# A hybrid decoder step on one core: stick-breaking prompt heads in pairs instead of one by one

## The reference

```python
def sb_attend(q, k, v, q_pos, k_pos, bias):
    z = (jnp.einsum('bqhd,bkhd->bhqk', q.astype(jnp.float32), k.astype(jnp.float32)) * SB_DH ** -0.5
         + bias.astype(jnp.float32)[None, :, None, None])
    valid = (k_pos[None, :] < q_pos[:, None])[None, None]
    log_stay = jnp.where(valid, jax.nn.log_sigmoid(-z), 0.0)
    after = lax.cumsum(log_stay, axis=3, reverse=True) - log_stay
    w = jnp.where(valid, jnp.exp(jax.nn.log_sigmoid(z) + after), 0.0)
    return jnp.einsum('bhqk,bkhd->bqhd', w, v.astype(jnp.float32))
```

## Time and profile before

| | before |
|---|---|
| median of 3 runs | 1431.58 us (1430.72 to 1433.55) |
| the profiled execution | 1428.48 us, of which 1426.7 us is the span from first to last instruction |
| PE busy, PEld busy | 91%, 87% of the span |
| DVE, ACT, POOL busy | 42%, 29%, 10% |
| mean granted TensorE clock | 0.935 of 2.4 GHz |
| prompt stick-breaking heads on PE | 600.65 to 697.31 us of the span |
| value products of the samples (L634) | 714.05 to about 741.5 us |

### The profile page before, as it was taken

One profiled execution on the slowest core, in us unless ns is written; L12 is line 12 of the kernel. 1 busy time (PEld: TensorE's weight loads), 2 busy tenths in 40 slices (PEclk: granted clock), 3 DMA queues, 4 the chain that ended last, 5 costly groups with the idle time before them and its releaser, 6 DMA issues.

```text
span 1426.7 us, 22310 instructions
## 1 busy us (share of the span) xinstructions
PE 1305.4 (91%) x9492; PEld 1242.0 (87%) x9492; DVE 604.6 (42%) x630; ACT 412.6 (29%) x462; POOL 149.1 (10%) x154
## 2 busy tenths in 40 slices
PE   5999999999977999889898869689999999999893
PEld 4999999999977999767586649679999999999893
DVE  5444312443345333255438632554442134433744
ACT  5222222222333111254311143432222222222442
POOL 6100000000113000100013301220000000001321
PEclk9999999999988999999857859899999999999997
DMA  5222223221230222201500002202222322222201
GB/s 182 89 88 81 67 89 118 89 88 56 77 134 30 88 88 91 92 30 45 177 0 18 22 10 77 88 30 88 88 74 89 103 89 89 77 68 91 90 30 63
DMA packets 36743, 109.98 MB, mean 77 GB/s; under 512 B 4626, under 2 KB 4642, under 8 KB 36562
## 3 DMA queue, kind: packets, MB, share of 16 engines
q1 hardware_dynamic: 34850, 103.10, 22.0%
q0 software_dynamic: 1232, 5.01, 1.1%
q10 hardware_dynamic: 608, 1.10, 0.2%
HBM read 103.57 MB, written 5.64 MB: 77 GB/s over the span
## 4 chain that ended last, share of the span: by engine, by line
PE 87%; DVE 7%; ACT 2%; issue 2%; POOL 0%; DMA 0%; ACTq 0%; POOLq 0%; DVEq 0%
PE PS L426 72%; PE PS L634 2%; DVE work L1118 2%; PE PS L682 1%; DVE x L1130 1%; PE PS L548 1%; DVE a_lo L1109 1%; PE PS L577 1%; PE PS L740 1%; PE PS L437 1%; PE PS L480 1%; PE PS L533 1%; PE PS L743 1%; PE PS L557 1%; PE PS L574 1%
## 5 line engine op out<-in xcount | busy, mean ns | idle before, releaser
L426 PE MATMUL PS<-a_hi,w_hi 128*128 128x272 f32 (+1 forms) x2064 | 432.6, 292 | 50.2 <-DVE a_lo L1109 22.8
L426 PE MATMUL PS<-a_lo,w_hi 128*128 128x272 f32 (+1 forms) x2064 | 431.3, 291 | 0.0
L426 PE MATMUL PS<-a_hi,w_lo 128*128 128x272 f32 (+1 forms) x2064 | 429.8, 290 | 0.0
L426 PEld LDWEIGHTS PS<-a_hi,w_hi 128*128 128x128 f32 (+1 forms) x2064 | 328.4, 191 | 57.9 <-issue 33.6
L426 PEld LDWEIGHTS PS<-a_hi,w_lo 128*128 128x128 f32 (+1 forms) x2064 | 328.2, 190 | 0.5
L426 PEld LDWEIGHTS PS<-a_lo,w_hi 128*128 128x128 f32 (+1 forms) x2064 | 326.0, 190 | 0.5
L1103 DVE TENSOR_TENSOR w_lo<-raw,w_hi 128x2048 fp32r<-128x2048 f32 (+2 forms) x97 | 201.6, 2078 | 229.5 <-ACT w_hi L803 229.5
L803 ACT ACTIVATE w_hi<-raw 128x2048 fp32r<-128x2048 f32 (+2 forms) x97 | 166.0, 1711 | 115.5 <-PE PS L426 115.4
L426 PE MATMUL PS<-h_lo,w_hi 128*128 128x272 f32 x704 | 145.2, 288 | 0.0
L426 PE MATMUL PS<-h_hi,w_lo 128*128 128x272 f32 x704 | 144.6, 287 | 0.0
L426 PE MATMUL PS<-h_hi,w_hi 128*128 128x272 f32 x704 | 144.5, 287 | 0.0
(11 more groups left out here) (272 smaller groups left out, 1072.2 us busy)
## 6 DMA issues: line engine op xcount, KB each, us to landing
raw<-in_f_in SPq DMA_DIRECT2D x86, 512.0 KB, 4.5
raw<-in_f_out SPq DMA_DIRECT2D x32, 384.0 KB, 3.3
raw<-in_w_in SPq DMA_DIRECT2D x24, 512.0 KB, 4.6
raw<-in_f_out SPq DMA_DIRECT2D x32, 320.0 KB, 3.1
raw<-in_w_out SPq DMA_DIRECT2D x8, 512.0 KB, 4.7
y<-in_cache_sb_k SPq DMA_DIRECT2D x16, 256.0 KB, 2.8
raw<-in_ple_w_gate SPq DMA_DIRECT2D x8, 512.0 KB, 4.6
x<-in_x SPq DMA_DIRECT2D x8, 272.0 KB, 7.1
```

The lines of the kernel that those rows point to most:

```text
L426: last = mm(PS[0:width, 4 * quad + 2 * c + half, 0:HALF], wt[:, slot, cols], act[:, k, half * HALF:(half + 1) * HALF], start=(k == 0 and n ...
```

## The change

Heads are taken in pairs p = 0 to 3.

- Logits: both heads' products read `proj` directly, head 2p in array rows 0 to 63 and head 2p+1 in rows 64 to 127, instruction by instruction in turn, into different banks. A pair's logits come in three units (diagonals; the 384 columns of key block 0; the 256 and 128 columns of blocks 1 and 2), and the units take the bank pairs (0, 1) and (2, 7) in turn. `q_pad` and GpSimd's copies are gone.
- Values: the products of the two heads alternate between the two column halves of the array, into the two halves of bank 3, which is copied out once for a pair.
- There are six `sb_z` buffers, and the weights are formed in place, so that `sb_w` is gone. One `sb_s` moves to the space that value pages 8 to 11 take later, and four value pages move to a free half of `raw`.
- Each page product is tied to a unit (`PAGE_UNIT`): samples 0 to 3 one in a unit, samples 4 and 5 together, 6 and 7 together.
- The orders of PE, ScalarE and VectorE are rewritten for pairs; SP waits at other points, and the second half of the `w_out` loads waits until all value pages are used. The load of the GLA state waits for the last pair's values.

```diff
-        sb_z = [scratch(dead, 1280 * n, [P, 1280]) for n in range(2)]
-        sb_s = [scratch(dead, 2560, [P, 1280]), scratch(extra_flat, 0, [P, 1280])]
-        sb_w = [scratch(extra_flat, 1280 * n, [P, 1280]) for n in (1, 2)]
+        spare = [hold_w[:, n, (at["out"][0] + 1) % 2, :] for n in range(2)]
+        sb_z = [scratch(dead, 1280 * n, [P, 1280]) for n in range(3)] + [scratch(spare[0], 0, [P, 1280])] + [
+            scratch(extra_flat, 1280 * n, [P, 1280]) for n in (1, 2)]
+        sb_s = [scratch(spare[1], 0, [P, 1280]), scratch(extra_flat, 0, [P, 1280])]
...
+        PAGE_UNIT = [(1, 1), (1, 2), (2, 1), (2, 2), (3, 1), (3, 1), (3, 2), (3, 2)]
+        raw_free = raw[:, at["out"][0] % 2, :]
+        v_page = [k_nat[:, c] for c in range(N_CH)] + [raw_free[:, c * 512:(c + 1) * 512] for c in range(4)] + [
+            spare[1][:, c * 512:(c + 1) * 512] for c in range(4)] + [v_nat[:, c] for c in range(N_CH)]
...
-                        sp.wait_ge(sig["z_full"], (j - 4) // N_PAGES + 3)
+                        p_, u_ = PAGE_UNIT[(j - 4) // N_PAGES]
+                        sp.wait_ge(sig["z_full"], 3 * p_ + u_ + 1)
...
+                        sp.wait_ge(sig["split_lo"], W0["out"] + 1)
+                    elif j == 8:
+
+                        sp.wait_ge(sig["c_full"], SB_HEADS - 1)
...
-                        sp.wait_ge(sig["o_full"], SB_HEADS)
+                        sp.wait_ge(sig["o_full"], SB_HEADS // 2)
...
+                    sp.wait_ge(sig["n_out"], DEC_BATCH * N_PAGES)
                     stage("out", 4, out_parts, first=2)
...
+            def prompt_z(p, u):
+
+                n = 3 * p + u
+                banks_ = ((0, 1), (2, 7))[n % 2]
+                k_, q_ = flat(proj[:, SK + p]), flat(proj[:, SQ + p])
+                if n >= 2:
+                    pe.wait_ge(sig["z_out"], n - 1)
+                if u == 0:
+                    blocks = [(j * P, j, j * P, (j + 1) * P) for j in range(4)]
+                elif u == 1:
+                    blocks = [(0, 0, P, SEQ)]
+                else:
+                    blocks = [(0, 1, 2 * P, SEQ), (256, 2, 3 * P, SEQ)]
+                for col, j, q0, q1 in blocks:
+                    for hh in range(2):
+                        r = slice(64 * hh, 64 * hh + 64)
+                        last = mm(PS[:, banks_[hh], col:col + q1 - q0], k_[r, j * P:(j + 1) * P], q_[r, q0:q1],
+                                  start=True, stop=True)
+                for at_, b in unit_pages(p, u):
+                    last = page_z(b, PS[:, banks_[at_], 384:448])
+                last.then_inc(sig["z_full"], 1)
...
+            def prompt_out(p):
+
...
                 for j in range(4):
-                    v_ = v_nat[:, j, h * SB_DH:(h + 1) * SB_DH]
-                    last = mm(out[:, j * P:(j + 1) * P], v_, w_[:, j * P:(j + 1) * P], start=(j == 0), stop=(j in (0, 3)))
-                    if j < 3:
-                        n = (3 - j) * P
-                        mm(out[:, (j + 1) * P:SEQ], v_, w_[:, off[j]:off[j] + n], start=(j == 0), stop=False)
+                    for wide in range(2 if j < 3 else 1):
+                        for hh in range(2):
+                            h = 2 * p + hh
+                            out, w_ = PS[64 * hh:64 * hh + 64, 3], sb_z[h % 6]
+                            v_ = v_nat[:, j, h * SB_DH:(h + 1) * SB_DH]
+                            if wide:
+                                n = (3 - j) * P
+                                last = mm(out[:, (j + 1) * P:SEQ], v_, w_[:, off[j]:off[j] + n], start=(j == 0), stop=False)
+                            else:
+                                last = mm(out[:, j * P:(j + 1) * P], v_, w_[:, j * P:(j + 1) * P], start=(j == 0),
+                                          stop=(j in (0, 3)))
                 last.then_inc(sig["o_full"], 1)
...
+            pairs = SB_HEADS // 2
+            for p, u in ((0, 0), (0, 1), (0, 2), (1, 0)):
+                prompt_z(p, u)
+            pe.wait_ge(sig["setup_new"], 1)
+            prompt_z(1, 1)
+            for p in range(pairs):
+                prompt_sums(2 * p)
+                if p + 1 < pairs:
+                    prompt_z(p + 1, 2)
+                if p:
+                    prompt_out(p - 1)
+                prompt_sums(2 * p + 1)
+                if p + 2 < pairs:
+                    prompt_z(p + 2, 0)
+                    prompt_z(p + 2, 1)
+            prompt_out(pairs - 1)
...
+            def logits(p, u):
+
+                n = 3 * p + u
+                banks_ = ((0, 1), (2, 7))[n % 2]
+                act.wait_ge(sig["z_full"], n + 1)
+                if u == 0 and p >= 3:
+                    act.wait_ge(sig["o_full"], p - 2)
+                first, width = ((0, 512), (512, 384), (896, 384))[u]
+                for hh in range(2):
+                    h = 2 * p + hh
+                    ins = fn(sb_z[h % 6][:, first:first + width], PS[:, banks_[hh], 0:width], ACT.Identity,
+                             bias=bias[:, h:h + 1], scale=SB_DH ** -0.5)
+                for at_, b in unit_pages(p, u):
+                    ins = page_logits(b, PS[:, banks_[at_], 384:448])
+                ins.then_inc(sig["z_out"], 1)
...
+            pairs = SB_HEADS // 2
+            for u in range(3):
+                logits(0, u)
...
+            log_part(1, sb_s[1])
+            logits(1, 0)
+            logits(1, 1)
+            for p in range(pairs):
+                if p + 1 < pairs:
+                    logits(p + 1, 2)
+                weight(2 * p, sb_z[2 * p % 6])
+                if p + 1 < pairs:
+                    log_part(2 * p + 2, sb_s[0])
+                weight(2 * p + 1, sb_z[(2 * p + 1) % 6])
+                if p + 2 < pairs:
+                    logits(p + 2, 0)
+                if p + 1 < pairs:
+                    log_part(2 * p + 3, sb_s[1])
+                if p + 2 < pairs:
+                    logits(p + 2, 1)
...
+            def masked(p):
+
+                dve.wait_ge(sig["z_out"], 3 * p + 1)
+                for hh in range(2):
+                    diag = sb_z[(2 * p + hh) % 6][:, 0:512].rearrange("p (j q) -> p j q", j=4)
+                    v.tensor_tensor(diag, diag, neg_diag[:].unsqueeze(1).broadcast_to([P, 4, P]),
+                                    ALU.add).then_inc(sig["z_masked"], 1)
...
+                z_ = sb_z[h % 6]
+                dve.wait_ge(sig["z_out"], 3 * (h // 2) + 3)
                 dve.wait_ge(sig["z_masked"], h + 1)
...
+                z_ = sb_z[h % 6]
                 dve.wait_ge(sig["c_full"], h + 1)
-                if h >= 2:
-                    dve.wait_ge(sig["o_full"], h - 1)
-                v.tensor_tensor(w_[:, 0:512], z_[:, 0:512], PS[:, 4, :], ALU.subtract)
-                v.tensor_tensor(w_[:, 512:1280].rearrange("p (a n) -> p a n", a=2),
+                v.tensor_tensor(z_[:, 0:512], z_[:, 0:512], PS[:, 4, :], ALU.subtract)
+                v.tensor_tensor(z_[:, 512:1280].rearrange("p (a n) -> p a n", a=2),
...
+            def pair_out(p):
+                dve.wait_ge(sig["o_full"], p + 1)
+                v.tensor_copy(flat(y[:, 4 + p])[:, 0:SEQ], PS[:, 3, :]).then_inc(sig["o_out"], 1)
...
+            masked(0)
             magnitudes(0)
+            magnitudes(1)
...
+            softplus(1, sb_z[1], sb_s[1])
+            masked(1)
+            for p in range(pairs):
+                exponents(2 * p)
+                if p + 1 < pairs:
+                    magnitudes(2 * p + 2)
+                if p >= 1:
+                    pair_out(p - 1)
+                if p + 1 < pairs:
+                    softplus(2 * p + 2, sb_z[(2 * p + 2) % 6], sb_s[0])
+                exponents(2 * p + 1)
+                if p + 1 < pairs:
+                    magnitudes(2 * p + 3)
+                if p + 2 < pairs:
+                    masked(p + 2)
+                if p + 1 < pairs:
+                    softplus(2 * p + 3, sb_z[(2 * p + 3) % 6], sb_s[1])
+            pair_out(pairs - 1)
...
-            pool.wait_ge(sig["d_ready"], SB_HEADS)
+            pool.wait_ge(sig["o_full"], SB_HEADS // 2)
```

More of the change, by code:

```diff
@@ L294, in embed_ticket, with unit_pages @@
             return T0["embed"] + s_ - 1 if s_ else T0["embed_first"]
+        def unit_pages(p, u):
+            return list(enumerate(b for b in range(DEC_BATCH) if PAGE_UNIT[b] == (p, u)))
         SPLIT_EARLY = ("f1_up0", "in", "f2_up0")
@@ L525, in _, with page_z @@
                 pe.wait_ge(psum_free[quad], (T0["merge"] + 1 - quad) // 2)
-            def prompt_z(h):
-                p = h // 2
-                k_, q_ = flat(proj[:, SK + p]), q_pad[h % 2]
-                pe.wait_ge(sig["z_out"], h)
-                pe.wait_ge(sig["q_pad_ready"], h + 1)
-                for j in range(4):
-                    mm(PS[:, 0, j * P:(j + 1) * P], k_[:, j * P:(j + 1) * P], q_[:, j * P:(j + 1) * P],
-                       start=True, stop=True)
-                mm(PS[:, 1, 0:384], k_[:, 0:P], q_[:, P:SEQ], start=True, stop=True)
```

(63 more changed lines are left out.)

47 lines of the change are left out of this document (10 added, 37 removed).

## The result

The changed kernel takes 1424.73 us in the median of 5 runs (1421.27 to 1425.03), the kernel before 1431.58 (1430.72 to 1433.96). The ratio is 0.9941 with a 95% interval of [0.9926, 0.9955]. A second series gave 1422.98 us and 0.9947 [0.9927, 0.9968]. The forecast was 1424.1 us. The profiled execution took 1421.75 us for a span of 1420.0, against 1428.48 and 1426.7.

A forecast was written before the change was run, and what follows sets the result against it. PE's own work was taken to bound the prompt heads. Stage -12.2 us with the start came to -16.0; clock falls gave back 8.5, leaving -7.5: 1431.6 to 1424.1 us. The forecast's own range was 1420 to 1428, overall 1417.5 to 1429.5.

The forecast's parts named there:

- Overlap at full rate: Prompt heads' logits and values: two half-array products overlap, so a pair costs what one head did.
- Both rivals without overlap: Only one direction overlaps: 1433.3 or 1432.9 us, chance 0.05; no overlap, slower: 1442 us, chance 0.04.
- Changes of mode: PE in the heads: each change between full and half array costs 0.15 us, 1.5 us in all.
- Waits: PE behind the first sums: waits covered before now lie open, 5.6 us in all.
- Start: Ahead of the first sums: logits start earlier, so these sums begin at 609.0 instead of 612.80, 3.8 us gained.
- Stage at an unchanged clock: From first sums to last values: 84.5 us before, 70.0 after, plus 2.3 for a slow sums(0).
- the cold sums(0): First head's sums come behind a wait and run at 1.2 GHz, adding 2.3 us.
- Clock: PE in the heads: five falls to the lower clock behind double page groups and waits, 1.7 us each, 8.5 us.
- After the stage: Behind the samples' new keys, what follows keeps its length within 1 us.
- Page loads and ACT: Later key-page loads stay covered, else 1 to 2 us; ACT's 0.4 us more per pair is covered.

The follow-up runs named there:

- second series: The changed kernel, unchanged, timed again beside versions with moved products: 1422.98 us, 0.9947 of the kernel before.
- the column order: Changed kernel with all seven value products of a pair's first head issued before the second head's, instead of alternating: 1428.4 us, ratio 0.9982.
- the direct logits: Kernel before, with single heads' logits reading their 64 rows straight from the projection and the padded copies removed: 1433.12 us, ratio 1.0009.
- the cut of the pages: Three quarters of the samples' page logits left out, in both kernels: changed kernel 1409.80 us, kernel before 1422.02 us.
- pages 5: Changed kernel with sample 5's page products moved inside sums(4): 1418.65 us, ratio 0.9912.
- the values moved: Changed kernel with the second pair's value products, and their copy on DVE, moved behind sums(5): 1422.12 us, ratio 0.9939.

## Why the prediction was right

- *Overlap at full rate*: right. Values 2.32 us a pair (2.4 expected). The three logits units took 2.59; 2.3 was forecast without the changes of mode, which these rows hold in part. Both rivals without overlap are out, and the column order shows what a lost overlap costs.
- *Changes of mode*: 0.15 us each estimated, 0.14 measured on the direct logits, where two come to 0.28.
- *Waits*: 1.8, 3.1 and 0.3 forecast behind sums(5), ahead of the last values and at sums(2); 1.74, 2.95 and 0.42 measured. Ahead of sums(7), where 0.4 was forecast, the last value product and the sums start 0.50 us apart against 0.32 in the middle: 0.2.
- *Start*: 16.64 - 12.67 = 3.97 us shorter, 3.8 forecast. Two terms were off and cancel: ACT began at 600.04 where 599.6 was forecast, and its six activations took 3.34 us where 3.7 was. In the second series' profiled execution the start took 13.55, so 0.9 us of this differs between executions.
- *Stage at an unchanged clock*: 80.45 less 8.5 for the clock and less 2.5 for the cold sums(0) is 69.5; my sum was 70.0.
- *Clock*: 8.5 us forecast as five short falls, 8.5 measured as three short ones and one of double length. The places were near the forecast ones: at sums(2), behind the first double page group, from within the second, and at the last values. The size is partly luck: in the second series' profiled execution the last stretch is missing and the double one is single, 5.1 us in all. The mechanism was incomplete. The prediction blamed waits and double page groups; the cut of the pages shows that the first three falls need the 8-column groups, and the direct logits show falls behind single groups with no wait, once the logits beside them use 64 rows. That the 64-row logits matter for the clock stood nowhere in the prediction.
- *After the stage*: the length to the output projection stayed within 0.1 us; 1 us of the 7.7 was given back behind it. The only group there that grew by more than 0.2 us is one of 96 products with `p_hi`, `p_lo`, 21.7 us busy against 19.8: a stretch at 0.50 lies in it (1330.90 to 1334.30), where the kernel before kept 1.00 from 1329.30 to 1345.50.
- *Page loads and ACT*: hidden, as costed. The loads showed when pages 5 were moved alone (1.75 us), and for 0.47 us with three quarters of the page products left out.

## What to carry to other kernels

Products that use half the rows or half the columns can be issued in alternation with those of the other half, and two then cost here what one did, weight loads included (2.32 us against 2.31). Before counting the gain, look at what will stand next to them: dense work that is taken out leaves narrow products and uncovered waits, and the clock took back 8.5 of the 16 us that the work and the start had won. Spread the narrow groups between dense ones and into the waits, and look at the order on the engine that releases the wait before moving PE's work into it.

## What the runs showed of the hardware

- Products of the other array half, float32 with two records each, start ahead of about four records of the running half that were issued before them. On row halves, units with runs of four records lost nothing (0.86 us) and a run of eight cost 0.55; on column halves, where longer runs met, three records of the second half started beside the last four of the first.
- A change between full array and row half costs 0.14 us at 2.4 GHz (a head of 11.10 us against 10.82, with two changes).
- PE busy without a gap doesn't keep the clock: with 64-row logits behind a page group, busy 3.10 of 3.10 us, it fell to 0.51, three times in one execution. The same groups beside 128-row logits kept 1.00 over 79.8 us. Whether the idle rows or the changes of mode matter isn't separated.
- The same program differs by 9 to 12 us from run to run (1427.46 to 1436.46 for the kernel before, 1412.04 to 1424.06 with the values moved), in step with its mean granted clock. Six runs gave intervals of about 0.2% to each side, 3 us, so smaller effects need more runs or a profiled stretch of their own.
